# Rounded halves of a matmul's input side by side, chunk by chunk, and the normed input on a 2 KiB boundary

## What is computed

```python
def first_block(x):                       # S5 and latent attention side by side, then a conv FFN
    a = rms_norm(x) @ w_in                # 2048 -> 1856
    x = x + concat(rms_norm(s5(a)), rms_norm(mla(a))) @ w_out
    a = conv3(rms_norm(x) @ w_up)         # 2048 -> 2 * 5632
    gate, val = split(a)
    return rms_norm(x + (silu(gate) * val) @ w_down)     # 5632 -> 2048

def second_block(h):                      # SSD and RWKV-7 side by side, then a gated FFN
    p = rms_norm(h) @ w_in_2              # 2048 -> 11744
    h = h + concat(ssd(p), rwkv7(p)) @ w_out_2           # 4096 -> 2048
    v = rms_norm(h)
    h = h + (silu(v @ w_gate) * (v @ w_up)) @ w_down     # 5632 each
    return rms_norm(h)
```

## Time and profile before

| | us |
|---|---|
| median of 3 runs | 2955.98 |
| lowest and highest run | 2952.76, 2956.33 |
| span of the profiled execution | 2954.4 |
| TensorE busy in it | 2857.8 (97%) |
| VectorE, ScalarE, GpSimd busy | 2039.6, 1552.7, 724.2 |

### The profile page before, as it was taken

The page is one execution under the profiler, slowest core; times in us unless marked ns, Lnnn a source line. Parts: engine busy times, 40 slices in busy tenths (PEclk is TensorE's granted clock), DMA queues, the critical chain, the costliest instruction groups (busy, mean ns, idle before and its releaser), DMA issues.

```text
span 2954.4 us, 52371 instructions
## 1 busy us (share of the span) xinstructions
PE 2857.8 (97%) x21074; PEld 2538.4 (86%) x21074; DVE 2039.6 (69%) x3273; ACT 1552.7 (53%) x2574; POOL 724.2 (25%) x870
## 2 busy tenths in 40 slices
PE   8989999999999998999899999999999999999998
PEld 8868988888888888888788888997888888888887
DVE  6675887765777667777777776777766665566654
ACT  7345555544555554566556655465445444444443
POOL 0342211200112230776456630003121110011112
PEclk9999999999999999999999999999999999999999
DMA  6314555556555555422222223454555555655554
GB/s 248 104 59 156 174 197 186 191 174 205 189 195 186 175 196 179 143 91 94 80 94 94 105 94 120 154 185 157 185 183 189 192 188 174 207 194 186 185 181 148
DMA packets 80046, 475.38 MB, mean 161 GB/s; under 512 B 8256, under 2 KB 11328, under 8 KB 38720
## 3 DMA queue, kind: packets, MB, share of 16 engines
q1 hardware_dynamic: 76768, 459.72, 45.0%
q10 hardware_dynamic: 3040, 12.32, 1.2%
HBM read 465.72 MB, written 6.29 MB: 160 GB/s over the span
## 4 chain that ended last, share of the span: by engine, by line
PE 78%; DVE 10%; ACT 4%; POOL 4%; issue 3%; DMA 0%; SPq 0%; POOLq 0%; ACTq 0%; DVEq 0%
PE bank L769 36%; PE bank L773 22%; PE bank L771 5%; PE bank L772 4%; PE bank L762 3%; DVE m L1307 2%; ACT m L2200 2%; POOL m L2933 2%; POOL m L2929 1%; DVE m L1353 1%; DVE m L1975 1%; PE bank L1103 1%; PE bank L1215 0%; PE bank L1107 0%; PE bank L866 0%
## 5 line engine op out<-in xcount | busy, mean ns | idle before, releaser
L773 PE MATMUL bank<-m,m 128*128 128x256 f32 x6624 | 1860.5, 281 | 0.0
L769 PE MATMUL bank<-m,m 128*128 128x512 f32 x4736 | 1650.0, 393 | 10.8 <-DVE m L2072 5.7
L1307 DVE TENSOR_TENSOR m<-m,m 128x1024 fp32r<-128x1024 f32 (+1 forms) x912 | 1033.1, 1141 | 569.9 <-ACT m L2200 563.5
L773 PEld LDWEIGHTS bank<-m,m 128*128 128x128 f32 x6624 | 1252.2, 189 | 0.2
L2200 ACT ACTIVATE m<-m 128x1024 fp32r<-128x1024 f32 (+1 forms) x912 | 877.7, 976 | 641.8 <-PE bank L773 615.4
L769 PEld LDWEIGHTS bank<-m,m 128*128 128x128 f32 x4736 | 890.7, 188 | 211.0 <-DVE m L2072 5.9
L771 PE MATMUL bank<-m,m 128*128 128x256 f32 x1888 | 561.2, 297 | 23.5 <-DVE m L1307 20.1
L772 PE MATMUL bank<-m,m 128*128 128x256 f32 x1888 | 534.6, 283 | 0.0
L771 PEld LDWEIGHTS bank<-m,m 128*128 128x128 f32 x1888 | 361.6, 192 | 43.4 <-issue 31.3
L772 PEld LDWEIGHTS bank<-m,m 128*128 128x128 f32 x1888 | 361.8, 192 | 1.3
L2909 POOL TENSOR_TENSOR m<-m,m 128x256 fp32r<-128x256 f32 x44 | 63.4, 1441 | 547.7 <-ACT m L2491 547.7
(11 more groups left out here) (375 smaller groups left out, 2830.5 us busy)
## 6 DMA issues: line engine op xcount, KB each, us to landing
m<-in_w_up SPq DMA_DIRECT2D x88, 1024.0 KB, 4.8
m<-in_w_down SPq DMA_DIRECT2D x128, 704.0 KB, 4.0
m<-in_w_gu SPq DMA_DIRECT2D x88, 1024.0 KB, 4.8
m<-in_w_out SPq DMA_DIRECT2D x48, 1024.0 KB, 5.1
m<-in_w_krv SPq DMA_DIRECT2D x48, 1024.0 KB, 4.8
m<-in_w_xbc SPq DMA_DIRECT2D x24, 1024.0 KB, 4.8
m<-in_w_z SPq DMA_DIRECT2D x16, 1024.0 KB, 4.8
m<-in_w_in SPq DMA_DIRECT2D x14, 1024.0 KB, 6.1
```

The source lines that it names most:

```text
L769: pe.matmul(bank.rearrange("p (a b) -> p a b", a=2), hi, x, start=kc == L.k0, stop=False)
L773: m = pe.matmul(ps, lo, x[:, 0, :], start=False, stop=last)
L1307: v.tensor_tensor(lo_of(k), raw_of(k)[0], hi_of(k).bitcast(F32), SUB).then_inc(*lo_v(("lo", k)))
```

## The change

The two halves of a chunk now stand next to each other. `hnr`, `far`, `vvr` and `ysr` become `[chunk, half, position]`, so that `x[:, 0:2, :]` of one chunk is one run of 2 KiB instead of two of 1 KiB. Every line that writes or reads a half has its two indices swapped. Before `hnr` is allocated, `top` is raised so that `hnr` begins at a multiple of 2048 bytes: 104 floats are left unused, and `hnr` and everything allocated after it moves up by 416 bytes. `hnr` then starts at byte 38912 (19 x 2048), `far` at 71680 (35 x 2048), `ysr` at 114496 (55 x 2048 + 1856). `ssr` keeps its order `[half, chunk, position]` and is only moved. The tiles before `hnr` (constants, `h`, scratch) and the weights' slots at the end stay where they were. No instruction is added, removed or put elsewhere on any engine.

```diff
         w12, omm = alloc(16), alloc(52)
+        top[0] += -(BASE // 4 + top[0]) % 512
         base = top[0]
         hno = top[0]
-        hnr = alloc(2, 16, T, dt=F32R)
-        hn_out = [(hnr[:, 0, i, :], hnr[:, 1, i, :]) for i in range(16)]
+        hnr = alloc(16, 2, T, dt=F32R)
+        hn_out = [(hnr[:, i, 0, :], hnr[:, i, 1, :]) for i in range(16)]
...
-        far = within(ffo, 2, 22, T, dt=F32R)
+        far = within(ffo, 22, 2, T, dt=F32R)
...
-            return far[:, :, kc % 22, :]
+            return far[:, kc % 22, :, :]
...
-        vvr = within(hno, 2, 16, T, dt=F32R)
-        ysr = within(sdo, 2, 16, T, dt=F32R)
+        vvr = within(hno, 16, 2, T, dt=F32R)
+        ysr = within(sdo, 16, 2, T, dt=F32R)
...
-            return hnr[:, :, kc, :]
+            return hnr[:, kc, :, :]
...
-            sums = linear(L_outr, lambda kc: vvr[:, :, kc - 16, :],
+            sums = linear(L_outr, lambda kc: vvr[:, kc - 16, :, :],
...
-            run(linear(L_outs, lambda kc: ysr[:, :, kc, :],
+            run(linear(L_outs, lambda kc: ysr[:, kc, :, :],
...
-                    a.activation(far[:, 0, j % 22, :], s, ACT.Copy).then_inc(*ffn_a(("hi", j)))
+                    a.activation(far[:, j % 22, 0, :], s, ACT.Copy).then_inc(*ffn_a(("hi", j)))
...
-                    g.tensor_tensor(far[:, 1, j % 22, :], s[:, 1, :], far[:, 0, j % 22, :].bitcast(F32), SUB).then_inc(*ffn_g(("lo", j)))
+                    g.tensor_tensor(far[:, j % 22, 1, :], s[:, 1, :], far[:, j % 22, 0, :].bitcast(F32), SUB).then_inc(*ffn_g(("lo", j)))
```

More of the change, by code:

```diff
@@ L676, in program @@
         N_ssd = [Norm(norms, [z[:, 4 * g + i, :] for i in range(4)], ("ssd_norm_g_2", 4 * g),
-                      [(ysr[:, 0, 4 * g + i, :], ysr[:, 1, 4 * g + i, :]) for i in range(4)], 512, 1e-5, 7)
+                      [(ysr[:, 4 * g + i, 0, :], ysr[:, 4 * g + i, 1, :]) for i in range(4)], 512, 1e-5, 7)
                  for g in range(4)]
@@ L2071, in halves_of_y @@
                         v.wait_ge(*ssd_a["vv", i])
-                        v.tensor_tensor(vvr[:, 1, i, :], yl[:, i, :], vvr[:, 0, i, :].bitcast(F32), SUB).then_inc(
+                        v.tensor_tensor(vvr[:, i, 1, :], yl[:, i, :], vvr[:, i, 0, :].bitcast(F32), SUB).then_inc(
                             *ssd_v(("vv", i)))
@@ L2490, in gate_up @@
                         a.wait_ge(*lin_pe["tile", L_down2[0].number(15)])
-                    a.activation(far[:, 0, j % 22, :], cvs2[j % 4], ACT.Copy).then_inc(*ffn_a(("hi2", j)))
+                    a.activation(far[:, j % 22, 0, :], cvs2[j % 4], ACT.Copy).then_inc(*ffn_a(("hi2", j)))
             shifts = [0]
@@ L2703, in halves_of_y @@
                     for i in range(8 * n, 8 * n + 8):
-                        a.activation(vvr[:, 0, i, :], yl[:, i, :], ACT.Copy).then_inc(*ssd_a(("vv", i)))
+                        a.activation(vvr[:, i, 0, :], yl[:, i, :], ACT.Copy).then_inc(*ssd_a(("vv", i)))
                     yield
@@ L2908, in gate_up @@
                     g.wait_ge(*ffn_a["hi2", j])
-                    g.tensor_tensor(far[:, 1, j % 22, :], cvs2[j % 4], far[:, 0, j % 22, :].bitcast(F32), SUB).then_inc(*ffn_g(("lo2", j)))
+                    g.tensor_tensor(far[:, j % 22, 1, :], cvs2[j % 4], far[:, j % 22, 0, :].bitcast(F32), SUB).then_inc(*ffn_g(("lo2", j)))
             def small(t):
@@ L2989, in pool_program @@
                 g.wait_ge(*ssd_a["vv", i])
-                g.tensor_tensor(vvr[:, 1, i, :], yl[:, i, :], vvr[:, 0, i, :].bitcast(F32), SUB).then_inc(
+                g.tensor_tensor(vvr[:, i, 1, :], yl[:, i, :], vvr[:, i, 0, :].bitcast(F32), SUB).then_inc(
                     *ssd_g(("vv", i)))
```

## The result

| | before | after |
|---|---|---|
| median of the runs, us | 2956.15 | 2971.24 |
| lowest and highest, us | 2952.76, 2957.81 | 2967.66, 2982.44 |
| span of the profiled execution, us | 2954.4 | 2968.3 |

The ratio on record is 1.006, with a 95% interval from 1.0041 to 1.0079; the two medians lie 15.1 us apart. The forecast was 2893 us with a range of 2845 to 2962, so the time lies above the range and on the other side. These four runs of the changed kernel span 14.8 us, the four before 5.1; but 13 runs of before in a later series span 14.4, so the wider spread alone says nothing of the change.

A forecast was written before the change was run, and what follows sets the result against it. TensorE's own matmul stream was taken to bound the kernel. 13.3 ns less on 4736 wide blocks, 63 us, took the span from 2954.4 to 2891.4; with 1.6 us from span to median, 2893 us, range 2845 to 2962.

The forecast's parts named there:

- What bounds the kernel: Wide stages, some 1640 us: only TensorE's own stream sets the pace; each ns of 4736 wide blocks is worth 4.7 us.
- What to compare with: L769 and L773 against plain float32 matmuls L762 and L926: 14 and 6 ns more for as many cycles of columns.
- Two runs become one, on a boundary: L769 in the wide blocks: the change saves 13.3 ns on each of 4736, 63 us.
- two rivals: Wide blocks: nothing changes, 2956 us, chance 0.28; or adjacency alone counts, gaining 31 us, 2924 us, chance 0.12.
- The piece of 64 bytes: Operand fetches, estimated as 16 floats: a run starting mid-piece touches 17 instead of 16, two runs 34 instead of 32.
- I take nothing for L773 and the narrow blocks: 256-column matmuls: no gain counted, the next weights' load sets their distance; upper bound 27 plus 32 us, kept in the range.
- the bound: Most that L773 and the narrow matmuls could gain, 5.6 ns each: 27 and 32 us, together 59 us.
- The other tiles' shift at nothing: Everything after `hnr`, moved by 416 bytes: activations and VectorE's operations cost nothing more.
- What is late next: Wide stages 3.8% shorter: VectorE at 82% and weight loads of 4.8 us in 5.3 both hold, so all 63 us arrive.
- The slower rival: `hnr` and `far` blocks: input stream meets the next weights' load worse, 355 instead of 346.7 ns, 36 us added, 2992; chance 0.18.
- the case on the border: Wide blocks: border and adjacency together bring the gain, 2893 us, own range 2834 to 2905; chance 0.42.
- What would show it: Profile after: L769's median at 379 instead of 391 ns, its distance 216 instead of 230, about 1200 records in 200 us.

The follow-up runs named there:

- e9: TensorE alone, computing nothing of the reference: one matmul with its weight load, 128 to 512 columns in several formats; 512 columns: fp32r 228.9 to 234.3 ns, bf16 215.8.
- e1: TensorE alone issuing the kernel's blocks, 32 variants of start, layout and form; 346.7 ns a block at before's `hnr` place, 348.9 to 353.5 at after's.
- e2: The changed kernel without the line that raises `top`: halves adjacent, `hnr` at byte 38496 as before; 2957.39 us, ratio 1.0002.
- e6: The changed kernel with all weights' slots moved down 96 bytes, restoring before's distance from input to weights modulo 256; 2954.08 us, ratio 0.9991.
- e4: TensorE alone, a grid of eight input starts by eight shifts of the low weights, 64 pairs; one pair ran at 340.0 ns in all groups.
- e5: TensorE alone: input starts in finer steps, all weights moved down, or fewer weight columns; 346.67 ns wherever input and weights kept the difference of start 96.
- e8: The changed kernel with low weights, `hnr`, `far` and `ysr` moved 64 bytes on modulo 256, the 340.0 ns places; 2932.16 us, ratio 0.9901.
- e10: The changed kernel again without an edit, one profiled execution; 2979.62 us.
- e11: The kernel before with only the raised `top` (halves apart, `hnr` at byte 38912), run again without an edit, one profiled execution; 2980.51 us.

## Why the prediction was wrong, step by step

**What bounds the kernel** was right. TensorE alone does, its stages have no waits, and a nanosecond of the wide block is 4.7 us: the table above has that rule for its first term, on eight executions.

**What to compare with** was right in its numbers and wrong in what it made of them. L769's 14 ns over L762 are there, and e9 gives the same in isolation (bf16 and float32 215.8, fp32r 229 to 234 for 512 columns). But "it grows with the runs, or with the columns" left two readings, and the sum took the first. A single contiguous run of 512 columns costs as much (e1: 234 ns apart and adjacent). The 5 to 6 ns for one run of 256 were too small besides: they are counted from L926's 111 ns, which is the 111.6 that e9 finds whether 128 or 192 columns stream, and above bf16's 109.2 with 256 columns the surcharge is 8 to 9 ns. L1072, which takes a pattern in two runs at the price of one, had said so; I gave it to two rivals instead of letting it decide.

**"Two runs become one, on a boundary"** is the step that failed, 4736 x 13.3 = 63 us. The adjacency is worth 0 (e2: before's counts and pace, 347.03 ns; e1: 346.7 both ways). The border is worth 0 as a border (e6) and cost 3.4 to 6.1 ns a block through the relation that it changed. The piece of 64 bytes was an estimate from one coincidence, 5 to 6 ns against 6.7 ns for 16 columns; e1, e4 and e5 show a period of 256 bytes and no advantage at multiples of 64: starts 0 and 128 are among the slowest. The argument for it, `ysr`'s 402 ns, was right that the place counts and wrong as evidence for borders: 38496 is as far off a 64-byte border as 114080 is, 32 bytes, and yet they differ by 7 ns. That could have been read from the numbers in the prediction itself.

**"I take nothing for L773 and the narrow blocks"** was nearly right. The narrow blocks' pace moved from 118.04 to 117.12 ns, 5.2 us of the 32 us that they had in the bound. The reason given was not: a floor that doesn't depend on the columns is there for 128 and 192 columns (111.6 both), but 256 columns take 117.3 to 118.6, 6 to 7 ns above it.

**The other tiles' shift at nothing** held: DVE 2039.6 to 2036.4 us, ACT 1552.7 to 1553.3. **What is late next** was never tried by after. In e8's stretch at 340.0 ns TensorE is idle for 0.12 us of 200 and VectorE busy for 155.95, so it holds there.

**The slower rival** (0.18) named the mechanism: the stream of the input meets the load of the weights, and the new place meets it worse, as `ysr`'s did. Its pace was right too, 355 ns against 353.3 measured. The whole term came out smaller: 36 us forecast, +15 in the medians, since 31% of after's blocks ran at 353.3 and 62% at 348.9 in the profiled execution; where 93% ran at 353.3 (e10), the time rose by 23.6 us. (The 8 ns a block were read from starts with two decimals; 353.3 less 346.7 is 6.6.) The earlier trace rows were both for it, while the case on the border stood on one of them and an estimate; the chances of 0.18 and 0.42 were too far apart.

**What would show it.** "If it stays at 391, the place of a run is not its price" was a sign too blunt to rely on: it went to 392 in one stretch, though the pace there had risen by 2.2 ns, and to 397 in the other. The distance from start to start told both apart. The matmuls in 200 us were 1134 instead of 1200. The sign given for the slower case, an L770 of 402 in the FFN, came as 397. L_out2's narrow blocks on `ssr`, meant to tell border from adjacency, tell neither. From 330 to 360 us, before, then after, then e10:

```profile
330.00:360.00 30.00, 30.00 (x259) 30.00 (x258) 29.62 (x44) 19.48 (x33) 11.98 (x10) 1.00 0.63 208
```

```profile
330.00:360.00 30.00, 30.00 (x267) 30.00 (x266) 29.62 (x44) 19.41 (x34) 11.99 (x10) 1.00 0.65 211
```

```profile
330.00:360.00 30.00, 30.00 (x257) 30.00 (x256) 29.65 (x43) 19.40 (x33) 13.20 (x11) 1.00 0.59 200
```

After did more matmuls there than before, 267 against 259, and its own repetition fewer, 257: a narrow block takes 350.0, 340.0 and 353.3 ns. Narrow blocks too, then, have two paces at one place. Read alone, the first would have passed for a gain of the border.

**What stays open.** Why the relation modulo 256 bytes sets the pace, and where in TensorE or SBUF fp32r's 13 ns arise. Both operands come from SBUF while one streams and the other loads, and the relation of their places matters; that they meet in a bank or a port is a guess that no run here tests. Also open is what decides which of two paces an interruption leaves behind, whether the interruption causes the change or only comes with it, and the 5.5 us by which e11 is longer than its pace and its clock say.

## What to carry to other kernels

Where TensorE streams without a wait, read the start-to-start pace for each stage and compare it between versions before anything else; a changed allocation can change it by 4% with every instruction in its place. Before crediting a layout or an alignment, repeat the change with the other operand moved by the same distance: if the effect goes, it was the relation. A stream of the real matmuls without the rest, tried at 16-byte steps of both operands, finds a good relation (here 1% of the kernel), and the kernel has to be run several times, since the pace it settles in differs from run to run. Before reading a difference of some us between two executions, compare their granted clocks too.

## What was not expected of the hardware

- An fp32r block of 512 + 256 columns with its two weight loads takes 340.0, 346.7, 353.3 or 360.0 ns, or a regular mixture of these, by the places of its operands modulo 256 bytes. The steps are 16 cycles at 2.4 GHz.
- At one and the same place it can hold either of two paces for hundreds of microseconds (348.9 or 353.3; 340.0 or 350.0), and where it changes an interruption stands, as short as 81 ns (622.58 us in after). e8's runs span 20.4 us, with its traces at 340.0 and 350.0.
- Kernels whose trace holds one pace spread too: e2's ten runs by 12.1 us, before's by 14.4. There the time goes largely with the granted clock, which was at its lower level for 60.4 us in e2's trace and 37.5 in e6's.
- fp32r costs 13.3 ns beyond its columns from 320 to 448 columns, 16 to 21 at 512, where bf16 costs 2.5 at 512. Loading 32 weight columns instead of 128 (108 ns instead of 188) doesn't lessen it.
